# Second block's attention issued head by head among the gate and convolution GEMMs

## What is computed

```
q, k, v, f_logit, c_b, c_c, c_in, gate_a, gate_c = split_cols(u @ w_in)
log_f  = log_sigmoid(f_logit + b_forget);  F = cumsum(log_f)
y_attn = softmax(q k^T / 8 + F[t] - F[s], causal) v @ w_attn_branch     # 8 heads of 64
y_conv = (c_b * short_conv(c_c * c_in, conv_w)) @ w_conv_branch
mixed  = (sigmoid(gate_a) * y_attn + sigmoid(gate_c) * y_conv) @ w_out
h      = h + rms_norm(mixed, g_mix_post)
```

## Time and profile before

| | |
|---|---|
| runs | 1503.60, 1494.61, 1492.95 us; median 1494.61 |
| profiled execution | 1500.17 us, its span 1498.4 us |
| mean granted clock of TensorE | 0.933 of full |
| PE busy | 1378.2 us, 92% |
| DVE, ACT busy | 797.2 us (53%), 637.0 us (43%) |
| chain that ended last | PE 83%, DVE 8%, ACT 4%, DMA 3% |

### The profile page before, as it was taken

How to read it: one execution, slowest core, us unless ns; L and a number is a source line. 1 busy time by engine, 2 the same in 40 slices (tenths; PEclk the granted TensorE clock), 3 DMA queues, 4 the chain that set the end, 5 groups by cost and what they waited for, 6 DMA issues and landing times.

```text
span 1498.4 us, 27068 instructions
## 1 busy us (share of the span) xinstructions
PE 1378.2 (92%) x11784; PEld 1250.4 (83%) x11784; DVE 797.2 (53%) x1039; ACT 637.0 (43%) x826; POOL 86.6 (6%) x79
## 2 busy tenths in 40 slices
PE   5579789999997988899999999998999799899998
PEld 3467689999984444799999999998999558899997
DVE  6962664434432248656654655545356625566643
ACT  4741363433343545454434544335344323644442
POOL 6531300000000011000000000000000000000000
PEclk9658899999999979999999999999999659999999
DMA  9506469985645570255556555454365104455452
GB/s 259 175 3 210 159 191 313 289 286 177 189 155 174 185 224 1 85 169 184 180 155 197 182 169 174 149 175 147 114 197 189 65 0 149 133 173 192 160 175 87
DMA packets 237797, 246.89 MB, mean 165 GB/s; under 512 B 5544, under 2 KB 233336, under 8 KB 237704
## 3 DMA queue, kind: packets, MB, share of 16 engines
q1 hardware_dynamic: 236968, 243.82, 51.1%
q0 software_dynamic: 480, 1.57, 0.6%
q10 hardware_dynamic: 256, 0.14, 0.0%
HBM read 244.47 MB, written 1.05 MB: 164 GB/s over the span
## 4 chain that ended last, share of the span: by engine, by line
PE 83%; DVE 8%; ACT 4%; DMA 3%; issue 1%; POOL 0%; SPq 0%; DVEq 0%; ACTq 0%
PE PS L1587 82%; DMA RING<-in_ada_w 1%; DVE WL L1016 1%; ACT PARTS L593 1%; PE PS L2124 1%; DMA RING<-in_w_out 0%; DMA RING<-in_w_attn_branch 0%; DVE ARENA L1211 0%; DMA RING<-in_w_in 0%; DVE ARENA L1214 0%; ACT ARENA L695 0%; DVE ARENA L1208 0%; DVE ARENA L1398 0%; DVE ARENA L1213 0%; DVE ARENA L1358 0%
## 5 line engine op out<-in xcount | busy, mean ns | idle before, releaser
L1587 PE MATMUL PS<-PARTS 128*128 128x256 f32 (+3 forms) x3480 | 834.1, 285 | 0.0
L1587 PEld LDWEIGHTS PS<-PARTS 128*128 128x128 f32 (+1 forms) x3480 | 610.3, 191 | 0.6
L1587 PE MATMUL PS<-HH,WL 128*128 128x256 f32 (+2 forms) x1896 | 544.7, 287 | 19.2 <-DVE PARTS L1005 7.9
L1016 DVE TENSOR_TENSOR WL<-RING,PARTS 128x2048 fp32r<-128x2048 f32 (+2 forms) x189 | 387.5, 2054 | 320.7 <-ACT PARTS L593 320.2
L1587 PE MATMUL PS<-HH,PARTS 128*128 128x256 f32 (+2 forms) x1896 | 542.4, 286 | 0.0
L593 ACT CAST PARTS<-RING 128x2048 fp32r<-128x2048 f32 (+2 forms) x189 | 323.6, 1715 | 312.6 <-DMA RING<-in_w_ffn_out 66.9
L1587 PEld LDWEIGHTS PS<-HH,WL 128*128 128x128 f32 x1896 | 362.8, 191 | 23.7 <-issue 13.0
L1587 PEld LDWEIGHTS PS<-HH,PARTS 128*128 128x128 f32 x1896 | 362.4, 191 | 0.4
L1587 PE MATMUL PS<-PARTS,WL 128*128 128x256 f32 (+1 forms) x768 | 219.0, 285 | 3.3 <-DVE WL L1016 3.3
L1587 PEld LDWEIGHTS PS<-PARTS,WL 128*128 128x128 f32 x768 | 147.0, 191 | 3.5 <-issue 3.5
L1587 PE MATMUL PS<-ARENA 128*32 128x63 f32 (+5 forms) x720 | 73.6, 302 | 11.5 <-DVE PARTS L1389 4.3
(11 more groups left out here) (296 smaller groups left out, 1149.7 us busy)
## 6 DMA issues: line engine op xcount, KB each, us to landing
RING<-in_w_ffn_in SPq DMA_DIRECT2D x44, 1024.0 KB, 5.1
ARENA<-in_ada_w SPq DMA_DIRECT2D x28, 1024.0 KB, 7.8
RING<-in_ffn_w_gate SPq DMA_DIRECT2D x22, 1024.0 KB, 5.4
RING<-in_ffn_w_up SPq DMA_DIRECT2D x22, 1024.0 KB, 5.3
RING<-in_ada_w SPq DMA_DIRECT2D x20, 1024.0 KB, 8.2
RING<-in_w_in SPq DMA_DIRECT2D x20, 1024.0 KB, 5.2
RING<-in_ffn_w_down SPq DMA_DIRECT2D x16, 768.0 KB, 4.4
RING<-in_w_ffn_out SPq DMA_DIRECT2D x16, 768.0 KB, 4.2
```

What stands on the lines that cost most here:

```text
L1016: V.tensor_tensor(WL[:, u % SLOTS, 0:w], RING[:, u % SLOTS, 0:w], WH[:, u % SLOTS, 0:w].bitcast(fp32), SUB)\
L1587: return nc.tensor.matmul(o, lhsT, rhs, start=start, stop=stop)
```

## The change

The order of the units becomes ... cin, gates, conv_br, attn_br, w_out (before: attn_br ahead of conv_br).

The forget tables are made in the second half of cin: behind unit 2 of cin PE waits for the forget row and does the FQ transposes, and behind each of the units 2 to 5 it does the matmuls of two heads, in banks 0 and 1, with DVE's FB instructions (`bias_tables`) behind its own `w_lows`. The row F is made one step later on DVE (i == 1).

The attention then runs in one loop with the GEMMs, eleven steps long: step i issues the scores of head i, the transposes of head i-2, the values of head i-3, and then one unit: gates 0 to 7 in steps 0 to 7, conv_br 0 and 1 in steps 8 and 9, nothing in step 10. DVE and ACT have loops of the same eleven steps. PSUM is laid out anew: scores in banks 0 and 1, transposes in 2 and 3, head outputs in 4, each gate unit in one bank (5 or 6, both halves), the first branch's output in halves of 5, 6 and 7. The sigmoids are two instructions of 128x2048 in steps 8 and 9 instead of eight of 128x512. CBH, CBL, O2H and O2L get storage of their own. attn_br 0 is issued with the k loop outside, so that each k waits only for its pair of heads.

```diff
+        CBH, at = arena(at, 4, SEQ, area=PARTS)
+        CBL, at = arena(at, 4, SEQ, area=PARTS)
+        O2H, _ = arena(LAYER_AT, 4, SEQ, area=PARTS)
+        O2L, _ = arena(LAYER_AT + 4 * SEQ, 4, SEQ, area=PARTS)
+        CONV_OUT = [PS[:, b, c:c + SEQ] for b, c in ((7, 0), (7, SEQ), (5, 0), (5, SEQ), (6, 0), (6, SEQ), (7, 0), (7, SEQ))]
...
+        stream("conv_br", w_view("w_conv_branch_2", 0), (0, 4), 0, D, 512)
         stream("attn_br", w_view("w_attn_branch_2", 0), (0, 4), 0, D, 512)
-        stream("conv_br", w_view("w_conv_branch_2", 0), (0, 4), 0, D, 512)
... ScalarE
-            for i in range(8):
-                act.wait_ge(S["gat_scaled"], i + 1)
-                nc.scalar.activation(GAT[:, 2 * i:2 * i + 2, :], GAT[:, 2 * i:2 * i + 2, :], ACT.Sigmoid).then_inc(S["gate_ready"], 1)
-                w_highs("gates", 4 + i)
+            for i in range(11):
+                if i < 10:
+                    w_highs("gates", i + 2)
+                if i < HEADS2:
+                    act.wait_ge(S["s2_max"], i + 1)
...                     (the two exponentials; then, for head i - 2, the copies of the transposes)
+                if i >= 4 and i % 2 == 0:
+                    k = (i - 4) // 2
+                    act.wait_ge(S["o2_ready"], 2 * k + 2)
+                    nc.scalar.copy(O2H[:, k, :], PS[:, 4, 0:SEQ]).then_inc(S["o2_hi"], 1)
+                if i == 4:
+                    act.wait_ge(S["conv_raw"], 1)
+                    nc.scalar.copy(CBH, SQ[:, 4:8, 0:SEQ]).then_inc(S["conv_hi"], 1)
+                if i in (8, 9):
+                    half = slice(KT, 2 * KT) if i == 8 else slice(0, KT)
+                    act.wait_ge(S["gat_scaled"], 8)
+                    nc.scalar.activation(GAT[:, half, :], GAT[:, half, :], ACT.Sigmoid).then_inc(S["gate_ready"], 1)
... VectorE
+            def bias_tables(h0):
+                if h0 == 0:
+                    dve.wait_ge(S["fq_ready"], 1)
+                    V.tensor_copy(FQ[:, :, :], PS[:, 3, 0:16].rearrange("p (a b) -> p a b", b=HEADS2)).then_inc(S["fq_copied"], 1)
+                for h in (h0, h0 + 1):
+                    dve.wait_ge(S["fb_ready"], h + 1)
+                    for at, keys in QT2:
+                        ins = V.scalar_tensor_tensor(FB[:, h, at:at + keys], PS[:, h % 2, 0:keys], -1.0,
+                                                     CN[:, C_TRI + at:C_TRI + at + keys], MUL, ADD)
+                    ins.then_inc(S["fb_copied"], 1)
             for i in range(4):
...
                 w_lows("cin", 4 + i)
+                if i >= 2:
+                    bias_tables(2 * i - 4)
             for c in range(2):
...
-                w_lows("cin", 8 + c)
+                bias_tables(2 * c + 4)
+            for i in range(11):
+                n, b = i % 3, 16 + 8 * (i % 3)
+                if i < HEADS2:
...                     (wait for the scores of head i; L1524's and L1529's instructions)
+                if 1 <= i <= 8:
+                    dve.wait_ge(S["unit_done"], AT["gates"] + i)
+                    V.tensor_tensor(GAT[:, 2 * i - 2:2 * i, :], PS[:, 5 + (i - 1) % 2, :].rearrange("p (a t) -> p a t", a=2), r_own, MUL)\
+                        .then_inc(S["gat_scaled"], 1)
+                if i >= 9:
+                    conv_mix(i - 9)
+                w_lows("gates", i + 2)
+                if i < HEADS2:
+                    dve.wait_ge(S["s2_exp"], i + 1)
...                     (reciprocal and scaling of head i; in steps 0 to 3 the convolution)
+                if i >= 4 and i % 2 == 0:
+                    heads2_low((i - 4) // 2)
+                if i == 5:
+                    dve.wait_ge(S["conv_hi"], 1)
+                    V.tensor_tensor(CBL, SQ[:, 4:8, 0:SEQ], CBH.bitcast(fp32), SUB).then_inc(S["conv_ready"], 1)
+            for c in range(2):
+                dve.wait_ge(S["unit_done"], AT["attn_br"] + c + 1)
+                dve.wait_ge(S["gate_ready"], 2)
...                     (products, sums and low parts as before, for the attention branch)
+                if c == 0:
+                    w_lows("w_out", 1)
... TensorE, in the loop over cin
+                if i == 2:
+                    pe.wait_ge(S["v2_copied"], 3)
+                    pe.wait_ge(S["f_ready"], 1)
...                     (the two transposes for FQ)
+                    for h in (2 * i - 4, 2 * i - 3):
+                        if h >= 2:
+                            pe.wait_ge(S["fb_copied"], h - 1)
+                        mm(PS[:, h % 2, 0:TALL], ident[0:HEADS2, h:h + 1].broadcast_to([HEADS2, P]), FROW[0:HEADS2, 5, :], True, True)\
+                            .then_inc(S["fb_ready"], 1)
...
+            pe.wait_ge(S["fb_copied"], HEADS2)
+            pe.wait_ge(S["u_ready"], 1)
+            for i in range(11):
+                if i < HEADS2:
+                    scores(i)
+                if 2 <= i <= HEADS2 + 1:
+                    turn(i - 2)
+                if i >= 3:
+                    values(i - 3)
+                if i == 1:
+                    pe.wait_ge(S["u_ready"], 2)
+                if i < 8:
+                    if i >= 2:
+                        pe.wait_ge(S["gat_scaled"], i - 1)
+                    linear3(AT["gates"] + i, [PS[:, 5 + i % 2, t * SEQ:(t + 1) * SEQ] for t in range(2)], own, SEQ)
+                elif i < 10:
+                    c = i - 8
+                    if c == 0:
+                        pe.wait_ge(S["conv_ready"], 1)
+                        pe.wait_ge(S["gat_scaled"], 7)
+                    else:
+                        pe.wait_ge(S["gat_scaled"], 8)
+                        pe.wait_ge(S["mix_part"], 2)
+                    linear3(AT["conv_br"] + c, CONV_OUT[4 * c:4 * c + 4], (CBH, CBL), SEQ)
+            u = AT["attn_br"]
+            split(u)
+            w = parts(u, 4, 512)
+            for k in range(4):
+                pe.wait_ge(S["o2_copied"], k + 1)
+                for t in range(4):
+                    ins = mm3(PS[:, t, 0:SEQ], [v[:, k, t * P:(t + 1) * P] for v in w], [v[:, k, :] for v in (O2H, O2L)], k == 0, k == 3)
+            ins.then_inc(S["unit_done"], 1)
+            pe.wait_ge(S["mix_part"], KT)
+            linear3(u + 1, list(range(4, 8)), (O2H, O2L), SEQ)
```

More of the change, by code:

```diff
@@ L1477, in _, with heads2_low @@
                     .then_inc(S["u_ready"], 1)
-                w_lows("cin", 8 + c)
+                bias_tables(2 * c + 4)
             dve.wait_ge(S["u_ready"], 2)
[L1480 to L1483, removed]
+            dve.wait_ge(S["fb_copied"], HEADS2)
+            def heads2_low(k):
+                dve.wait_ge(S["o2_hi"], k + 1)
+                V.tensor_tensor(O2L[:, k, :], PS[:, 4, 0:SEQ], O2H[:, k, :].bitcast(fp32), SUB).then_inc(S["o2_copied"], 1)
@@ L2082, in _ @@
                 linear3(AT["cin"] + i, [4 + 2 * (i % 2), 5 + 2 * (i % 2)], own if i < 2 else conv, SEQ if i < 2 else TCONV)
-            pe.wait_ge(S["v2_copied"], 3)
-            pe.wait_ge(S["f_act"], 1)
-            for i in range(8):
-                if i >= 2:
-                    pe.wait_ge(S["gat_scaled"], i - 1)
-                linear3(AT["gates"] + i, [2 * (i % 2), 1 + 2 * (i % 2)], own, SEQ)
-            pe.wait_ge(S["f_ready"], 1)
-            pe.wait_ge(S["gat_scaled"], 8)
-            for qt in range(2):
-                t0 = NMETA + qt * P
-                ins = nc.tensor.transpose(PS[:, 3, qt * HEADS2:(qt + 1) * HEADS2], FROW[0:HEADS2, 5, t0:t0 + P],
-                                          ident[0:HEADS2, 0:HEADS2])
@@ L2138, in _ @@
-            for c in range(2):
-                if c == 0:
-                    pe.wait_ge(S["s2_sb"], HEADS2)
-                linear3(AT["attn_br"] + c, list(range(4 * c, 4 * c + 4)), (O2H, O2L), SEQ, first=("o2_copied", 0) if c == 0 else None)
-            pe.wait_ge(S["conv_ready"], 1)
-            for c in range(2):
-                pe.wait_ge(S["mix_part"], 4 * c + 4)
-                linear3(AT["conv_br"] + c, list(range(4 * c, 4 * c + 4)), (CBH, CBL), SEQ)
+                if i == 2:
+                    pe.wait_ge(S["v2_copied"], 3)
+                    pe.wait_ge(S["f_ready"], 1)
+                    for qt in range(2):
+                        t0 = NMETA + qt * P
+                        ins = nc.tensor.transpose(PS[:, 3, qt * HEADS2:(qt + 1) * HEADS2], FROW[0:HEADS2, 5, t0:t0 + P],
+                                                  ident[0:HEADS2, 0:HEADS2])
+                    ins.then_inc(S["fq_ready"], 1)
@@ new lines, in _, with scores @@
+                if i >= 2:
+                    for h in (2 * i - 4, 2 * i - 3):
[3 more added lines that the diff above has]
+                            .then_inc(S["fb_ready"], 1)
+            def scores(h):
+                p, m = h % 2, h // 2
+                r = slice(64 * p, 64 * p + 64)
+                if h >= 2:
+                    pe.wait_ge(S["s2_sb"], h - 1)
+                for qt, (at, keys) in enumerate(QT2):
```

(21 more changed lines are left out.)

168 lines of the change are left out of this document (44 added, 124 removed).

## The result

| | before | after |
|---|---|---|
| median of the runs | 1493.78 us | 1478.72 us |
| lowest, highest | 1491.60, 1503.60 | 1470.86, 1482.73 |
| ratio, 95% interval | | 0.9892 [0.9855, 0.9929] |
| profiled execution, its span | 1500.17, 1498.4 us | 1482.73, 1480.9 us |
| mean granted clock | 0.933 | 0.943 |

The change wins 15 us, about 1.1%. It was forecast to win 29. The stated range, 1456 to 1480 us, just holds the result; the case's own range of 1458 to 1475 did not.

What follows compares the result with a forecast made beforehand. PE, busy 92% of the span, was taken as the bound. Terms 11.7 + 68.2 + 22.4 + 0.8 + 3.5 + 5.7 = 112.3 us against 142.05, less small waits: 29.4 us gained, 1465 us; range 1456 to 1480, case's own 1458 to 1475.

Steps and rivals of the forecast that it cites:

- The stage before the loop: Cin's second half up to gate 0: tables 4.0, idle 4.6, clock 2.3, last FB wait 0.8, together 11.7 us.
- The wait behind cin 3: PE waits for head 0's FB behind DVE's low part: idle about 4.6 us (3.5 to 6), then half clock.
- The head: One attention head in the loop: 2.8 us instead of 5.46, so 22.4 us for eight (21.8 to 25.1).
- The units: Eight gate, two conv_br and two attn_br units on PE at 5.68 us each: 68.2 us.
- The covers: In the loop, loads and DVE and ACT work fit within steps of 8.5 us; waits there cost nothing.
- the last pair: At attn_br 0, the last head pair's low part comes late: 0.7 us of stall, put at 0.8.
- w_out 0 in two pieces: First half of k starts at once, second after a 2.0 us gap (1.3 to 3); clock adds 1.5 us.
- the base of the sum: Before, from 1123.47 to w_out 0's end: 142.05 us, with a head at 5.46 us at clock 0.50.
- the chain: Rival in the loop: DVE's weight and softmax work makes steps 10 us, adding 12 us: 1477 us; chance 0.11.
- a few falls of the clock: Rival: clock falls in two or three loop steps, or cin's gap costs more: 8 to 15 us, 1473 to 1480; 0.08.
- The half clock in every step: Rival in the loop: the clock falls in each attention slice, costing 48 us: 1514 us; chance 0.05.
- the buffers: Rival: heads wait for copies from single buffers in banks 2 to 4, leaving some 10 us gain: 1485 us; 0.04.

Runs made afterwards that it cites:

- e1: The changed kernel run again with nothing changed: 1480.73 us, ratio 0.9924 to the kernel before.
- e5: The kernel before, unchanged, run for a second profile of it: 1488.85 us, one execution.
- e6: The kernel before, unchanged, run for a third profile of it: 1490.02 us, one execution.
- e4: The kernel before with 48 extra unused matmuls right ahead of its attention, nothing interleaved: 1496.07 us, ratio 1.0027.
- e3: Changed kernel with DVE's forget tables ahead of low parts and cin's last product, split table waits, last pair's low part ahead of w_out 0's: 1469.69 us, 0.9844.
- e9: The same program as e3, run once more: 1467.81 us, ratio 0.9846 to the kernel before.

## Why the prediction was right in sign and wrong in size

**The stage before the loop** was forecast 11.7 us longer than the plain end of cin. It is 1112.90 to 1143.12 less 0.90 us of scores, 29.3 us, where before 17.4 passed from cin 2's end to gate 0: 11.9. The wait behind cin 3, its cause (DVE's low part ahead of the tables) and the half clock behind it are as told; the idle was 3.0 us (4.75 in e1), not 4.6. That the sum came so near is luck in part, since its terms missed in both directions: idle 3.0 and 0.9 us for 4.6 and 0.8, the clock 3.4 (0.67 over 10.21 us) for 2.3, and the 4.7 that remain, tables and changes of kind, for 4.0.

**The head** was put at 2.8 us between 2.73 and 3.14; it is 2.96. That is 1.3 us over eight heads.

**The units** were put at 5.68 us; beside attention the gates take 5.85 (1167.47 to 1173.31 in the changed kernel is 5.84). At a change of kind a matmul starts 0.21 to 0.23 us before its successor, not 0.12, in both directions. Over the eight gate units and the two of conv_br (5.75 each) that is 1.5 us, where I had put 0.3 for all changes.

**The covers** held: no wait of PE inside the loop, loads and low parts in time, the last pair 0.42 us late (0.8 forecast; the two attn_br units with it 12.4 us against 12.2), w_out 0 in two pieces with 1.87 us between them (2.0 forecast; with its clock 9.8 us against 9.2). One more fall of the clock, at the first gate unit, was not in the sum: that unit took 7.48 us, 1.6 more than the others.

Together these are 0.2 + 1.3 + 1.5 - 0.3 + 0.2 + 0.6 + 1.6 = 5.1 us: the section after was forecast at 159.4 - 29.4 = 130.0 us and was 135.0. That is 5 us of the miss.

**The step that failed is the base of the sum.** I priced the attention of before by one trace at 5.46 us per head at clock 0.50 and took 142.05 us, up to w_out 0's end, as what the program takes. e5 and e6 show the clock rising by itself inside that attention, as it did in e4, and a section of 149.1 us instead of 159.4. That is 10.3 us of gain against one kind of execution, seen in one profile of three; 7.0 of them lie in the tables and the attention, the rest in the branch unit and w_out 0 behind them. I saw that the profiled execution was 5.56 us above the median and moved both times by it, as if the difference lay elsewhere. It lay in the very stretch that I priced: of the 11.3 us by which that execution is longer than e5's, the section holds 10.3. With 149.1 the sum would have been 19 us, with the terms as measured 14, and the medians gave 15. So the mechanism was right: light work in series with the GEMMs, a head at nearly half its price because the clock holds, and the waits gone. The price of the kernel before was not, and that the result still lies inside the range is luck: the range had been widened for the chain, which did not come, and for a few falls of the clock, of which one short one came in the loop.

**The rivals.** The half clock in every step did not come: 1.00 in the loop in all eight profiles of kernels that have it, behind its first unit. Its argument was weaker than I thought, since the clock does rise in the attention of before in two of three profiles. On the Trainium skill's statement in TensorE: Matmul & The Clock Gate, Part 4: PE-mode transpose, that transposes do not count as PE work for the full clock: these runs do not show it as an obstacle, attention with five transposes in every head went along with a rise at 1210.6 us in e5. The same page says in its Part 1, of a kernel's start, that how many matmuls run at the low clock varies between runs of the same kernel. These runs show such a spread in the middle of a kernel: no rise in one execution of before and a rise in two, and e3 and e9, one program, at 1.00 and 0.79 in the same unit. The chain and the buffers did not bind either: DVE is busy 22.62 us of 35.27 in the full steps.

## What to carry to other kernels

Interleaving light matmuls with a dense GEMM on the same engine hid none of them here (8.82 us a step is 2.96 of attention and 5.85 of gate unit); it removed waits and kept the clock at its upper level. The gain is worth only what the light stretch really loses, averaged over executions. Before pricing a stretch by its granted clock, take a second and third profile, or read how much of it the median shows. In an in-order list, put small work that another engine waits for ahead of work whose own input is still on its way: that swap of two lines was worth 6 us in the section, nearly half of what the whole change brought there. And compare programs by parts of the trace only as far as two profiles of one program agree: the sections of e3 and e9 differ by 3.0 us.

## What the hardware showed that I had not expected

The attention with 64-row operands, fully busy, ran at 0.50 for 25 us and longer in one execution, and rose to 1.00 some 37.5 us from the forget tables on in two others (at 1210.6 in e5, 1212.0 in e6), with no change in the instructions.

The fall is as uncertain: 0.39 us of idle between light matmuls was followed by 0.79 in e9 and by 1.00 in e3, and 0.87 us, in one program, by 0.82 in the changed kernel's profile and by 1.00 in e1.

The clock in the first block (0.79 to 0.90 from 100 to 220 us) goes with arrivals 900 us later that lie up to 13 us apart, nearly as much as the change is worth.

A matmul's start to start grows from 0.12 to 0.21 to 0.23 us where 64-row or transposing operations meet the GEMM's 128-row ones; a gate unit between them takes 5.85 us instead of 5.68.
